# An expert layer's gate and up products computed in two row halves of the array

## The reference, cut to what matters

```python
def _expert_choice_ffn(h, w_router, w_gate, w_up, w_down):
    cap = CAP_FACTOR * N // N_EXPERTS                 # 128 and 64 tokens an expert
    aff = jax.nn.softmax(jnp.einsum('nd,de->ne', h, w_router).astype(jnp.float32), axis=-1)
    gate, idx = lax.top_k(aff.T, cap)
    xe = h[idx]
    hid = jax.nn.silu(jnp.einsum('ecd,edf->ecf', xe, w_gate)) * jnp.einsum('ecd,edf->ecf', xe, w_up)
    ye = jnp.einsum('ecf,efd->ecd', hid, w_down) * gate[..., None].astype(h.dtype)
    return jnp.zeros_like(h).at[idx.reshape(-1)].add(ye.reshape(-1, D))
```

## Time and profile before

| | |
|---|---|
| median of 3 runs | 2539.5 us (2539.25 to 2540.68) |
| profiled execution, its own time | 2536.96 us |
| its span, first to last instruction | 2535.2 us |
| PE busy | 2458.3 us, 97% |
| VectorE busy | 1683.0 us, 66% |
| ScalarE busy | 1472.2 us, 58% |
| mean granted clock of TensorE | 0.987 |

### The profile page before, as it was taken

The page is one execution under the profiler, slowest core; times in us unless marked ns, Lnnn a source line. Parts: engine busy times, 40 slices in busy tenths (PEclk is TensorE's granted clock), DMA queues, the critical chain, the costliest instruction groups (busy, mean ns, idle before and its releaser), DMA issues.

```text
span 2535.2 us, 42579 instructions
## 1 busy us (share of the span) xinstructions
PE 2458.3 (97%) x16082; PEld 2201.6 (87%) x16082; DVE 1683.0 (66%) x2550; ACT 1472.2 (58%) x2081; POOL 161.2 (6%) x165
## 2 busy tenths in 40 slices
PE   8999999989949999999999999999999999999997
PEld 7888867667739999898999989899998989999896
DVE  6354279954677666676766667676666767666676
ACT  4333278877645556565555656555565655556574
POOL 0000000000010101011010101101010110101010
PEclk9999999999969999999999999999999999999999
DMA  5343254454456767676676767667676766767695
GB/s 187 109 140 110 73 173 158 143 198 138 137 200 232 253 232 245 230 253 229 248 252 232 245 231 253 230 245 254 231 243 231 254 230 245 253 233 243 230 321 214
DMA packets 99668, 542.37 MB, mean 214 GB/s; under 512 B 11072, under 2 KB 15552, under 8 KB 49408
## 3 DMA queue, kind: packets, MB, share of 16 engines
q1 hardware_dynamic: 92192, 515.30, 57.7%
q0 software_dynamic: 7392, 25.96, 4.6%
HBM read 500.32 MB, written 40.89 MB: 213 GB/s over the span
## 4 chain that ended last, share of the span: by engine, by line
PE 70%; DVE 1%; DMA 0%; issue 0%; ACT 0%; POOL 0%; DVEq 0%; ACTq 0%; POOLq 0%
PE ex_gate_ps L1854 16%; PE ex_up_ps L1854 16%; PE ex_gate_ps L1856 7%; PE ex_up_ps L1856 7%; PE ex_up_ps L1868 2%; PE ex_down_ps L1868 2%; PE ex_down_ps L1869 2%; PE ex_down_ps L1870 2%; PE ex_down_ps L1871 2%; PE ex_up_ps L1870 2%; PE ex_up_ps L1872 2%; PE ex_down_ps L1872 2%; PE ex_up_ps L1869 2%; PE ex_up_ps L1871 2%; PE ex_turn_ps L1829 1%; PE ex_turn_ps L1831 0%
## 5 line engine op out<-in xcount | busy, mean ns | idle before, releaser
L1706 DVE TENSOR_TENSOR ex_w_lo<-ex_w,ex_w_hi 128x2048 fp32r<-128x2048 f32 x384 | 879.9, 2292 | 460.4 <-ACT ex_w_hi L1623 459.0
L1623 ACT ACTIVATE ex_w_hi<-ex_w 128x2048 fp32r<-128x2048 f32 x384 | 733.4, 1910 | 221.3 <-PE ex_down_ps L1872 106.9
L1854 PE MATMUL ex_gate_ps<-ex_xt,ex_w_hi 128*128 128x384 f32 x2048 | 594.1, 360 | 1.5 <-DVE ex_xt L1712 1.5
L1854 PE MATMUL ex_up_ps<-ex_xt,ex_w_hi 128*128 128x384 f32 x2048 | 592.1, 359 | 0.0
L1856 PE MATMUL ex_gate_ps<-ex_xt,ex_w_lo 128*128 128x192 f32 x2048 | 513.7, 251 | 0.0
L1856 PE MATMUL ex_up_ps<-ex_xt,ex_w_lo 128*128 128x192 f32 x2048 | 512.7, 250 | 0.0
L1856 PEld LDWEIGHTS ex_gate_ps<-ex_xt,ex_w_lo 128*128 128x128 f32 x2048 | 392.5, 192 | 0.6
L1856 PEld LDWEIGHTS ex_up_ps<-ex_xt,ex_w_lo 128*128 128x128 f32 x2048 | 391.2, 191 | 0.0
L1854 PEld LDWEIGHTS ex_gate_ps<-ex_xt,ex_w_hi 128*128 128x128 f32 x2048 | 385.9, 188 | 2.3 <-issue 1.7
L1854 PEld LDWEIGHTS ex_up_ps<-ex_xt,ex_w_hi 128*128 128x128 f32 x2048 | 384.6, 188 | 0.0
L1641 ACT ACTIVATE ex_gate_low<-ex_gate_ps 128x384 f32<-128x384 f32 x128 | 63.0, 492 | 208.2 <-PE ex_gate_ps L1856 208.2
(11 more groups left out here) (316 smaller groups left out, 4057.1 us busy)
## 6 DMA issues: line engine op xcount, KB each, us to landing
ex_w<-in_w_experts SPq DMA_DIRECT2D x384, 1024.0 KB, 4.8
pj_w<-in_w_in SPq DMA_DIRECT2D x54, 512.0 KB, 3.6
at_bias<-in_near_bias SPq DMA_DIRECT2D x8, 1536.0 KB, 9.4
at_v_near<-v_scratch SPq DMA_DIRECT2D x24, 256.0 KB
o_scratch<-ld_out SPq DMA_DIRECT2D x24, 256.0 KB, 6.2
q_p<-in_x SPq DMA_DIRECT2D x12, 512.0 KB, 4.3
acc_scratch<-k_p SPq DMA_DIRECT2D x12, 512.0 KB, 5.1
h_scratch<-q_p SPq DMA_DIRECT2D x12, 512.0 KB, 2.9
```

The source lines that it names most:

```text
L1623: act.activation(w_hi[:, c % SLOTS, :], w[:, c % SLOTS, :], ACT.Copy).then_inc(hi_w, 1)
L1706: dve.tensor_tensor(w_lo[:, c % SLOTS, :], w[:, c % SLOTS, :], w_hi[:, c % SLOTS, :].bitcast(F32), ALU.subtract).then_inc(lo_w, 1)
L1854: nc.tensor.matmul(out[:, b, 0:2 * CAP], w_hi[:, slot, f], xt[:, k, :, :].rearrange("p h c -> p (h c)"), start=k == 0, stop=False)
```

## The change

Each matmul of a gate or up chunk becomes two of 64 rows: rows 0 to 63 of the contraction slice with weights from partitions 0 to 63, and rows 64 to 127 with the others. Each goes into a bank of its own, so gate and up take four banks each, all eight. The two halves are added afterwards: ScalarE's copy and VectorE's first add have twice the columns, and VectorE makes one more add. The buffer `up_sum` is gone. The banks that the down product and the turned tokens had to themselves are now pieces of `gate_ps` and `up_ps`, with waits for it.

```diff
-        gate_low = sb("ex_gate_low", [P, BLOCKS, CAP])
-        up_low = sb("ex_up_low", [P, BLOCKS, CAP])
+        gate_low = sb("ex_gate_low", [P, BLOCKS, 2, CAP])
+        up_low = sb("ex_up_low", [P, BLOCKS, 2, CAP])
...
-        gate_ps = ps("ex_gate_ps", [P, BLOCKS, WIDE])
-        up_ps = ps("ex_up_ps", [P, BLOCKS, WIDE])
-        down_ps = [ps(f"ex_down_ps{i}", [P, WIDE]) for i in range(2)]
-        turn_ps = [ps(f"ex_turn_ps{i}", [P, WIDE]) for i in range(2)]
-        y_ps = [[down_ps[0][:], down_ps[1][:]], [up_ps[:, 0, :], up_ps[:, 1, :]]]
+        gate_ps = ps("ex_gate_ps", [P, BLOCKS, 2, WIDE])
+        up_ps = ps("ex_up_ps", [P, BLOCKS, 2, WIDE])
+        turn_ps = [gate_ps[:, 0, i, :] for i in range(2)]
+        y_ps = [[out[:, i, :] for i in range(2)] for out in (gate_ps[:, 1], up_ps[:, 0])]
+        ROW_HALVES = [slice(i * P // 2, (i + 1) * P // 2) for i in range(2)]
...
-                        act.activation(gate_low[:], gate_ps[:, :, CAP:2 * CAP], ACT.Copy).then_inc(gate_lowered, 1)
+                        act.activation(gate_low[:], gate_ps[:, :, :, CAP:2 * CAP], ACT.Copy).then_inc(gate_lowered, 1)
...
-                        dve.tensor_tensor(gate_sum[:], gate_ps[:, :, 0:CAP], gate_low[:],
+                        dve.tensor_tensor(gate_low[:], gate_ps[:, :, :, 0:CAP], gate_low[:], ALU.add).then_inc(paired, 1)
+                        dve.wait_ge(paired, e * 2 * SPANS + 2 * gate_of(c) + 1)
+                        dve.tensor_tensor(gate_sum[:], gate_low[:, :, 0, :], gate_low[:, :, 1, :],
                                           ALU.add).then_inc(gate_summed, 1)
...
-                            nc.tensor.matmul(out[:, b, 0:2 * CAP], w_hi[:, slot, f],
-                                             xt[:, k, :, :].rearrange("p h c -> p (h c)"), start=k == 0, stop=False)
-                            last = nc.tensor.matmul(out[:, b, 0:CAP], w_lo[:, slot, f], xt[:, k, 0, :],
-                                                    start=False, stop=k == DT - 1)
+                            for i, rows in enumerate(ROW_HALVES):
+                                nc.tensor.matmul(out[:, b, i, 0:2 * CAP], w_hi[rows, slot, f],
+                                                 xt[rows, k, :, :].rearrange("p h c -> p (h c)"), start=k == 0,
+                                                 stop=False)
+                            for i, rows in enumerate(ROW_HALVES):
+                                last = nc.tensor.matmul(out[:, b, i, 0:CAP], w_lo[rows, slot, f], xt[rows, k, 0, :],
+                                                        start=False, stop=k == DT - 1)
...
+                        if c == UP_CHUNKS:
+                            pe.wait_ge(gate_summed, spans + SPANS)
...
+                    if c == W_CHUNKS - 1 and not last:
+                        pe.wait_ge(s_scaled, halves + 1 + START)
+                        pe.wait_ge(y_summed, halves + 1 + START)
```

More of the change, by code:

```diff
@@ L1414, in experts @@
         xt = sb("ex_xt", [P, DT, 2, CAP], F32R)
-        gate_low = sb("ex_gate_low", [P, BLOCKS, CAP])
-        up_low = sb("ex_up_low", [P, BLOCKS, CAP])
+        gate_low = sb("ex_gate_low", [P, BLOCKS, 2, CAP])
+        up_low = sb("ex_up_low", [P, BLOCKS, 2, CAP])
         gate_sum = sb("ex_gate_sum", [P, BLOCKS, CAP])
         silu = sb("ex_silu", [P, BLOCKS, CAP])
-        up_sum = sb("ex_up_sum", [P, BLOCKS, CAP])
         hid = sb("ex_hid", [P, BLOCKS, CAP])
@@ L1438, in experts @@
         last_ss, last_mean, last_rt, last_rs = (sb(f"fi_last_{n}", [P, 2]) for n in ("ss", "mean", "rt", "rs"))
-        gate_ps = ps("ex_gate_ps", [P, BLOCKS, WIDE])
-        up_ps = ps("ex_up_ps", [P, BLOCKS, WIDE])
-        down_ps = [ps(f"ex_down_ps{i}", [P, WIDE]) for i in range(2)]
-        turn_ps = [ps(f"ex_turn_ps{i}", [P, WIDE]) for i in range(2)]
-        y_ps = [[down_ps[0][:], down_ps[1][:]], [up_ps[:, 0, :], up_ps[:, 1, :]]]
+        gate_ps = ps("ex_gate_ps", [P, BLOCKS, 2, WIDE])
[3 more added lines that the diff above has]
+        ROW_HALVES = [slice(i * P // 2, (i + 1) * P // 2) for i in range(2)]
         ch = Choice(sem, sb("ch_turned_sb", [P, 2, 2 * PROMPT_AT]), sb("ch_mine", [P, 2, EXPERTS]),
-                    sb("ch_span", [P, 2, EXPERTS]), down_ps[0])
+                    sb("ch_span", [P, 2, EXPERTS]), up_ps[:, 1, 0, :])
         const_in = sem("ex_const_in")
@@ L1451, in experts @@
         chunk_done = sem("ex_chunk_done")
+        paired = sem("ex_paired")
         gate_lowered, gate_summed, gated = sem("ex_gate_lowered"), sem("ex_gate_summed"), sem("ex_gated")
@@ L1462, in experts @@
         released = sem("ex_released")
-        pe_released = sem("ex_pe_released")
         gathered_s, gathered_p = sem("ex_gathered_s"), sem("ex_gathered_p")
@@ L1640, in expert @@
                     if gate_of(c) is not None:
-                        act.activation(gate_low[:], gate_ps[:, :, CAP:2 * CAP], ACT.Copy).then_inc(gate_lowered, 1)
+                        act.activation(gate_low[:], gate_ps[:, :, :, CAP:2 * CAP], ACT.Copy).then_inc(gate_lowered, 1)
                     if up_of(c) is not None:
-                        act.activation(up_low[:], up_ps[:, :, CAP:2 * CAP], ACT.Copy).then_inc(up_lowered, 1)
+                        act.activation(up_low[:], up_ps[:, :, :, CAP:2 * CAP], ACT.Copy).then_inc(up_lowered, 1)
                     if c in DOWN_STEP and last:
@@ L1732, in expert @@
                         dve.wait_ge(up_lowered, spans + n + 1)
-                        dve.tensor_tensor(up_sum[:], up_ps[:, :, 0:CAP], up_low[:],
+                        dve.tensor_tensor(up_low[:], up_ps[:, :, :, 0:CAP], up_low[:], ALU.add).then_inc(paired, 1)
+                        dve.wait_ge(paired, e * 2 * SPANS + 2 * n + 2)
+                        dve.tensor_tensor(hid[:], up_low[:, :, 0, :], up_low[:, :, 1, :],
                                           ALU.add).then_inc(up_summed, 1)
@@ L1736, in expert @@
                         dve.wait_ge(gated, spans + n + 1)
-                        dve.tensor_tensor(hid[:], up_sum[:], silu[:], ALU.mult).then_inc(hidden, 1)
+                        dve.tensor_tensor(hid[:], hid[:], silu[:], ALU.mult).then_inc(hidden, 1)
                     if c in DOWN_STEP and last:
@@ L1902, in expert @@
                         pe.wait_ge(lo_x, (e + 1) * FILLS + 1)
-                        pe.sem_inc(pe_released, 1)
+                        pe.sem_inc(released, 1)
                         turn_x(2)
```

## The result

The changed kernel takes 2606.66 us (median of 4 runs, 2600.02 to 2609.68) against 2539.38 us (4 runs, 2538.95 to 2540.68): a ratio of 1.026 with a 95% interval of 1.0247 to 1.0273, or +67.3 us. The forecast was +12.8 us. The sign and the range held; the size didn't, and most of it comes from the rival that had been given 0.07, instruction fetch.

The account below looks back on a forecast made before the run. PE, busy 97% of the span, was taken as the bound. Terms 4.1 + 6.2 + 2.5 = 12.8 on 2537.0 gave 2549.8; with the runs' median 2.5 higher, 2552 us (+0.5%), range 2515 to 2620.

Parts of the forecast that it names:

- instruction fetch: PE's expert loop, grown to about 2,450 instructions, is refetched at each branch back: say +30 us, 2582; chance 0.07.
- The step: Gate and up matmul pairs, 384 plus 192 columns: nothing vanishes, second half starts 1 ns later, 4096 times: +4.1 us.
- The rival of vanishing loads: Gate and up steps: weight loads hide beneath the other half's matmul, gain 61 us, about 2491; chance 0.18.
- halves that disturb each other: Gate and up steps: a load stretches both halves' streams, +110 us, 2660, or half of it, 2605; chance 0.13.
- The change of form: PE switches between halves and the whole-array down product twice an expert: 16 x 0.39, +6.2 us.
- VectorE, 0 us: Gate and up sums: wider and second adds cost 1.92 us a pair of chunks, hidden under PE's up chunk: 0 us.
- The last expert: Chunks 14 to 16 of the last expert start about 0.1, 0.6 and 1.8 us late as VectorE scales tiles: +2.5 us.

Follow-up runs that it names:

- e1: Changed kernel with PE's loop over fifteen experts written out, so PE has no branch back; 2549.08 us (1.0036).
- e3: Changed kernel with whole 128-row matmuls, contraction slices 0 to 3 into one bank and 4 to 7 into the other, same sums; 2543.95 us (1.0016).
- e5: Kernel before, without halves, with two experts in a turn of PE's loop (2,852 instructions, six branches back); 2562.59 us (1.0093).
- e9: Changed kernel with only chunks 0 to 3 in halves (loop of 1,686) and 128 semaphore increments ahead of the loop; 2567.69 us (1.0115).
- e12: Changed kernel with only chunks 0 and 1 in halves (loop of 1,558) and 50 semaphore increments ahead of the loop; 2549.27 us.
- e4: Changed kernel with chunks 0 to 7 in halves and 8 to 15 in whole matmuls by slices (1,942 instructions); 2610.68 us (1.0271).

## Why the prediction was right and wrong

**The step, +4.1 us.** Right that nothing of it vanishes and that halves run side by side; the 1 ns for the second half's later start was not there. By the starts in e1's trace a chunk lasts as long as before, 4.55 us, and the second half's records lie 3 to 15 ns behind without lengthening anything. The rival of vanishing loads, chance 0.18, got nothing, and so did that of halves that disturb each other.

**The change of form, +6.2 us.** Right. In e1 it costs 0.20 us into and 0.17 us out of halves, 0.37 an expert against 0.39, so 5.9; by the times, e1 less e3 is 5.1 us.

**VectorE, 0 us.** Right that it is hidden. The busy time rose by 1918.2 - 1683.0 = 235 us, forecast 246; the wide add took 0.957 us, forecast 0.96, and ScalarE's copy 0.814, forecast 0.82.

**The last expert, +2.5 us.** Gate and up of the sixteenth expert take 1.8 us longer than those of the others in e1 (74.77 against 72.99), and 1.1 us of idle time at L1874 stands in the row above. By the starts in e3's trace, chunks 14, 15 and 16 of the last expert begin 0.17, 0.48 and 1.9 us late, where the prediction had 0.1, 0.6 and 1.8. e3 has no halves, and the kernel before has no such delays, so they belong to the sums and banks; that a late sum of VectorE is the cause is argued, not shown.

**Instruction fetch, 0 in the sum and a rival at 0.07.** This step failed, twice.
- The chance. The earlier trace rows had proved that a loop can stay, which shows no more than that 1,427 instructions fit. The next sentence had the new loop at 2,450. The forecast let a size that the rows didn't cover count as covered, where the one figure at hand, the 2,048 instructions that the prediction took from the Trainium skill ("Runtime: NRT & Kernel Launch", section Instruction fetch mechanics), was exceeded. This had to be the forecast itself, and the rest of the terms an addition to it.
- The price, "15 x 0 to 4.3 us, say +30". The bound was the landing of a 64 KB transfer, taken as the whole wait, with nearly all of it under the branch's lead of 4.2 us. But the branch took 6.07 us and the engine needs some more until it runs, so 2.4 us lie bare (33.6/14), not 0.1. And a gap has consequences. In the traces e1 and the changed kernel lie 62 us apart (spans 2545.9 and 2607.9). Some 38 us of it are gaps (33.6 + 3.9), and the rest stands behind them: stretches at half the clock as at 1321.3, in seven turns and 27 us in all, of which half is lost, so 14; and seven turns in which the gate and up chunks last 4.64 us instead of 4.55, about 10 us in all. The same sum holds for e5: 14.6 us of gaps, three stretches of 3.4 us at half the clock, so 5, and two turns with slow chunks, so 3, give 23 of its 23 us. What sets these slower chunks is open: they come after some gaps, but e9, which has no fetch in its later turns, has them from the fourth chunk on as well (some 1.1 us a turn more than e12).

With the terms as measured the sum would have been 3.5 (sums and banks, the last expert among it) + 5.1 (form) + 57.6 (loop) = 66.2 us. The terms that were in the sum came to 8.6 of the 12.8 forecast. That 2606.66 us lies in the range at all is in part luck: the fetches had been priced to 2582, and the range reached 2620 for other rivals as well, which did not happen.

No version measured here beats the kernel before: the halves without their loop trouble, e1, are still 0.36% slower, since they give nothing back.

## What to carry to other kernels

Before a change that multiplies the instructions in an engine's hardware loop, count them in blocks of 256 from where the loop begins: PE kept seven blocks. By that count, which was tried with loops of 1,427 to 2,852 instructions on PE alone, up to 1,537 (six blocks and one) stay wherever they lie, more than 1,792 never do, and in between a few instructions ahead of the loop decide. A lost loop cost 4 to 8 us at each return, most when a border lies just behind the loop's first instruction; written out straight, the same instructions cost nothing. In a profile it shows as many "instruction" packets, a branch of 6 us and idle time released by "issue" at the loop's first instruction.

## What was unexpected of the hardware

- A loop's place is worth as much as its length: 2552.44 us with 95 instructions ahead, 2668.24 us with 90.
- Gaps of 2.1 to 3.5 us in a PE that is otherwise busy were in many turns (seven of fourteen in the changed kernel) followed by 3.4 us or more at a granted clock of 0.50, half speed for longer than the gap itself.
- Matmuls can stay in a step of 0.290 us instead of 0.284 for whole turns, with whole and with half matmuls (e4, e9), without a wait in the profile; the cause is open.
